# Opening of a two-block model on one core: k/v weight chunks moved to even distance among the adaLN chunks

## What is computed

```python
shift, scale, gate = jnp.split(jax.nn.silu(c) @ ada_w[l] + ada_b[l], 3, axis=-1)
shift_c, scale_c, gate_c = jnp.split(jax.nn.silu(c_ctx) @ ada_w[l] + ada_b[l], 3, axis=-1)
h = rmsnorm(x, norm_g[l]) * (1.0 + scale[:, None]) + shift[:, None]
hc = rmsnorm(xc, norm_g[l]) * (1.0 + scale_c) + shift_c
qc, kc, vc, upc, ufc, gc = split_proj(hc @ w_in[l])
q, k, v, up, uf, g = split_proj(h @ w_in[l])
```

## Time and profile before

| | |
|---|---|
| median of three runs | 2354.19 us (2352.36 to 2354.57) |
| the profiled execution, its own time | 2351.8 us |
| its span in the trace | 2350.0 us |
| TensorE busy | 2269.2 us (97%) |
| VectorE / ScalarE / GpSimd busy | 1290.6 / 1040.8 / 267.9 us |
| HBM read and written | 428.89 MB and 6.29 MB |
| mean granted clock of TensorE | 0.988 |

### The profile page before, as it was taken

How to read it: one execution, slowest core, us unless ns; L and a number is a source line. 1 busy time by engine, 2 the same in 40 slices (tenths; PEclk the granted TensorE clock), 3 DMA queues, 4 the chain that set the end, 5 groups by cost and what they waited for, 6 DMA issues and landing times.

```text
span 2350.0 us, 30042 instructions
## 1 busy us (share of the span) xinstructions
PE 2269.2 (97%) x11859; PEld 1831.6 (78%) x11859; DVE 1290.6 (55%) x2038; ACT 1040.8 (44%) x1602; POOL 267.9 (11%) x326
## 2 busy tenths in 40 slices
PE   5899999999999999999999998999999999999998
PEld 2477777777777866678888886888888888888887
DVE  3354533332332264545776767677755777567764
ACT  2233333332322254445554465555544555345553
POOL 1000100000010122100020324111100111001111
PEclk8999999999999999999999999999999999999999
DMA  9964433444655485734566544565555555656553
GB/s 355 349 241 166 149 126 114 137 138 161 244 179 171 135 280 178 244 99 159 182 199 206 171 152 153 179 194 182 189 195 191 185 186 186 197 188 188 187 189 117
DMA packets 322427, 437.14 MB, mean 186 GB/s; under 512 B 13848, under 2 KB 220112, under 8 KB 321264
## 3 DMA queue, kind: packets, MB, share of 16 engines
q1 hardware_dynamic: 316800, 413.19, 53.3%
q0 software_dynamic: 3392, 16.90, 1.9%
q10 hardware_dynamic: 2096, 5.15, 0.6%
HBM read 428.89 MB, written 6.29 MB: 185 GB/s over the span
## 4 chain that ended last, share of the span: by engine, by line
PE 88%; DVE 4%; ACT 3%; DMA 2%; issue 1%; POOL 1%; SPq 0%; ACTq 0%; POOLq 0%
PE ps L1332 24%; PE ps L1333 12%; PE ps L1307 9%; PE ps L1309 9%; PE ps L1308 9%; PE ps L1327 5%; PE ps L1329 5%; PE ps L1328 5%; PE ps L1287 3%; PE ps L1381 1%; ACT SPL L1538 1%; DVE SPL L1781 1%; PE ps L1398 1%; DMA RAW<-in_w_in_dram 1%; DMA RAW<-in_ada_w_dram 1%
## 5 line engine op out<-in xcount | busy, mean ns | idle before, releaser
L1781 DVE TENSOR_TENSOR SPL<-RAW,SPL 128x1024 fp32r<-128x1024 f32 x592 | 752.7, 1274 | 618.3 <-ACT SPL L1538 615.6
L1332 PE MATMUL ps<-HS,SPL 128*128 128x512 f32 x2688 | 954.4, 400 | 12.3 <-DVE SPL L1781 9.5
L1538 ACT ACTIVATE SPL<-RAW 128x1024 fp32r<-128x1024 f32 x592 | 622.1, 1055 | 492.3 <-PE ps L1309 171.6
L1333 PE MATMUL ps<-HS,SPL 128*128 128x256 f32 x2688 | 755.5, 281 | 0.0
L1332 PEld LDWEIGHTS ps<-HS,SPL 128*128 128x128 f32 x2688 | 507.2, 189 | 135.8 <-DVE SPL L1781 8.4
L1333 PEld LDWEIGHTS ps<-HS,SPL 128*128 128x128 f32 x2688 | 510.4, 190 | 2.0 <-issue 1.7
L1307 PE MATMUL ps<-SPL,HS 128*128 128x512 f32 x960 | 398.5, 415 | 15.5 <-POOL HS L2232 5.6
L1309 PE MATMUL ps<-SPL,HS 128*128 128x512 f32 x960 | 379.3, 395 | 0.0
L1308 PE MATMUL ps<-SPL,HS 128*128 128x512 f32 x960 | 379.1, 395 | 0.0
L1307 PEld LDWEIGHTS ps<-SPL,HS 128*128 128x128 f32 x960 | 183.3, 191 | 78.8 <-issue 24.7
L1308 PEld LDWEIGHTS ps<-SPL,HS 128*128 128x128 f32 x960 | 183.6, 191 | 41.5 <-issue 6.0
(11 more groups left out here) (281 smaller groups left out, 1684.9 us busy)
## 6 DMA issues: line engine op xcount, KB each, us to landing
RAW<-in_w_in_dram SPq DMA_DIRECT2D x208, 512.0 KB, 5.7
RAW<-in_ada_w_dram SPq DMA_DIRECT2D x192, 512.0 KB, 4.9
RAW<-in_ffn_w_up_dram SPq DMA_DIRECT2D x192, 512.0 KB, 3.5
RAW<-in_w_out_dram SPq DMA_DIRECT2D x96, 512.0 KB, 4.4
RAW<-in_ffn_w_down_dram SPq DMA_DIRECT2D x96, 512.0 KB, 3.8
x_spill<-XT POOLq DMA_DIRECT2D x2, 2048.0 KB, 15.1
XT<-x_spill POOLq DMA_DIRECT2D x1, 4096.0 KB, 16.9
MM<-in_x_dram ACTq DMA_DIRECT2D x2, 1024.0 KB, 11.0
```

The lines of the kernel that those rows point to most:

```text
L1332: mm(PS[b][:, :], wr, hh, start=k == 0, stop=False, skip_group_check=True)
L1333: m = mm(PS[b][:, 256:512], wl, hh[:, 0:256], start=False, stop=k == KT - 1, skip_group_check=True)
L1538: act(SPL[:, (n - 1) % NSPL, 0, :], raw_of(i), ACT.Copy).then_inc(s_hi, 1)
L1781: tt(w[:, 1, :], raw_of(s["i"]), w[:, 0, :].bitcast(F32), ALU.subtract).then_inc(s_lo, 1)
```

## The change

The k/v chunks of steps 1 to 3 are put after the eighth and the sixteenth adaLN chunk of a step in place of the twelfth and the sixteenth. (`cs` holds sixteen adaLN chunks; `kv[2u - 1:2u]` stands after all of them in both versions.) They come to stand at 24 and 33, 42 and 51, 60 and 69, 70 and 71: eight adaLN chunks between any two of the first six. The number of side steps popped with every second adaLN chunk, which was 2 for chunks 0 to 7, 4 for 8 to 27 and 2 from 28 on, becomes 4 from chunk 8 on.

```diff
                 if c.shape == 0:
-                    pop_side((2 if i < 8 or i >= 28 else 4) if c.group.side == 2 and c.kc % 2 == 0 else 0)
+                    pop_side((2 if i < 8 else 4) if c.group.side == 2 and c.kc % 2 == 0 else 0)
...
                 cs[-1].then = start_h
-                return cs[:12] + kv[2 * u - 2:2 * u - 1] + cs[12:] + kv[2 * u - 1:2 * u] if u else cs
+                return cs[:8] + kv[2 * u - 2:2 * u - 1] + cs[8:] + kv[2 * u - 1:2 * u] if u else cs
```

## The result

The kernel after takes 2363.43 us (median of five runs, 2361.82 to 2367.48), the kernel before 2354.19 us: a ratio of 1.0046, with a 95% interval of 1.0035 to 1.0057, or 9.2 us more. The profiled execution of the kernel after took 2363.4 us, its span is 2361.6 us. One execution of this study, of the kernel after with the old number of side steps, took 3236 us at a granted clock of 0.65 and is left out of all figures.

The account below looks back on a forecast made before the run. TensorE was taken to bound the kernel, so an opening shift passes to the end one for one. Terms -0.5 + 2.9 + 9.7 = +12.1 us gave 2366 us; range 2352 to 2371 us.

Parts of the forecast that it names:

- Rival A: Opening: cycle as computed, but the clock drops only for kv0 and at most once more; +0.4 to +4.3 us, chance 0.20.
- Rival C: Opening's end set by something both kernels have, the spill or the h tiles; shift below 2 us, 2354, chance 0.09.
- kv0: First k/v chunk, moved from 28 to 24: lands at 52.1 us, starts at 55.7 in place of 59.92.
- The cycle: Eight adaLN chunks, one k/v chunk: next k/v chunk starts 7.6 us after the eight begin; 13.76 us per cycle.
- the landing: Restarted w_in load, issue to landing: 4.1 us taken, bounded below by 3.7.
- The lower bound of 3.7: Least landing time from 20 to 130 us; at it the five cycles would give 2.0 us back.
- kv5 without the clock: Start of kv5 with no clock effect: 124.5 us against 125.02 before, -0.5 us.
- The clock: Drops at six idle times of 3.8 us or more, ahead of kv0 to kv5: 2.9 plus 9.7, 12.6 us.
- the tail: After kv5 (h tiles of step 3, kv6, kv7, copies out): same list in both versions, so its length stays.
- kv5 near 137 us: Sign in the profile after that would show the forecast right: kv5 near 137 us.
- At nothing: Terms priced at zero in the opening, among them four side steps in place of two.
- Rival B: DMA stream closes up if restart loads land in 2.5 us; kv5 starts at 115.3, -8 us, 2346, chance 0.15.

Follow-up runs that it names:

- the second profile: Profile of the kernel after run once more, unchanged, beside three others: 2362.03 us, ratio 1.0043 against the kernel before.

## Why the prediction was right

The forecast was +12.1 us and 2366 us; measured were +9.2 and 2363.4. The sign and the mechanism stand, and each link of the chain is in the trace; two of its terms and one of its grounds were off. The range, 2352 to 2371 us, was wide enough to hold rivals A and C too, so it is the steps that count. By those steps, against the trace after:

- *kv0* was put at 55.7 us and started at 56.02, behind the seventh high part of the h tiles as said.
- *The cycle.* From the start of the eight adaLN chunks to the next k/v chunk I had 7.6 us. Measured were 7.27, 7.18, 7.43, 7.16 and 6.99, 7.2 in the mean. The term that was off is the landing: 4.1 taken, 3.50 to 3.95 measured. The lower bound of 3.7 was the better one in this execution; in the kernel after with the old number of side steps they took 3.73 to 4.04. That these loads find the engines idle, where the one of 4.1 us had a share of 0.57 around it, does not explain it: in the run with matmuls in the idle time, loads that were issued behind a microsecond with a share of 1.06 and 0.96 landed in 3.72 and 3.69 us, one behind a share of 0.00 in 3.85, and two behind 1.07 and 0.50 in 4.71 and 4.36. So 4.1 us lies within the scatter, and its cause stays open. The estimate of 3.2 us from the Trainium skill, page "DMA: Bandwidth & Descriptors", section "Anatomy of one DMA", which the page gives for the GpSimd path, is too low for these loads of SyncE. Over the five cycles that is -2.0 us, and kv0's start gives 0.3 back: kv5 without the clock at 133.16 - 10.3 = 122.9 in place of 124.5.
- *The clock* was the main term, 12.6 us. Over 6.16 us, kv0 to kv4 took 2.0, 2.8, 1.6, 2.5 and 1.5 us more, 10.3 together, and kv5 to kv6 took 10.05 us, 2.6 more than before: 12.9. The run with matmuls in the idle time shows the cause. The forecast of six drops came true in this execution, but its ground did not: I had six idle times of 3.8 us or more, each longer than the one of 3.74 us that came with a drop, and four of the five ahead of kv1 to kv5 are shorter than that (3.34 to 3.63 us). That the clock dropped at all of them is in part luck; the second profile has four drops in six.
- *What I left out*: the drop that the kernel before has from 134.5 to 138 us lies in the tail, which I had called the same in both. It is not there in the profile after: from kv6 to the mark it takes 13.1 us in place of 14.7. That is -1.6 us. It is no work of the change: the kernel after with the old number of side steps has 15.0 us there, the kernel before with the new number 13.1, behind the same two idle times of 1.2 and 0.6 us. So that this execution was spared it is luck; a row with its price was there, and the sum had it at nothing in both kernels.
- *The sum* of what was measured: 122.9 - 125.0 = -2.1, +10.3, +2.6, -1.6, in all +9.2 us, and the mark moved by 9.1. I also wrote "kv5 near 137 us", where my own terms give 124.5 + 2.9 + 4 x 1.9 = 135.0; it came at 133.2.
- *At nothing* were the side steps: both runs on them show it.
- Rival A (the clock holds) is out, though a single execution can come halfway to it. Rival B (the stream closes up) is what the kernel does as soon as it has the buffers: kv5 starts at 116.0 us where 115.3 was worked out, and the total is 2345.8 where it was 2346, though B reached its numbers by a shorter landing and not by more buffers. With eight buffers its point of decision is not reached, 3.5 us being the least landing time and 2.5 what it asked. Rival C is out, the mark moved by the whole loss.

On the clock the Trainium skill, page "TensorE: Matmul & The Clock Gate", section "HAM oscillation", says that a loop which waits for its next slice falls back to the low clock in each round. The trace after agrees with it in all five rounds from kv1 to kv5, the second profile in three of five.

## What to carry to other kernels

With a ring of n load buffers, look at what frees the buffer of the item that is on the critical path: here the k/v chunk stood n + 1 places behind the last one, so its own load was gated by the first thing TensorE does after the last one, and even spacing was the bad spacing; distances of eight and ten by turns were no better, though, and what helped was one buffer more. A wait of a few microseconds ahead of a block of large matmuls cost its own length here and, where the clock dropped, 1.3 to 2.9 us more in the block behind it. Before moving work between resources, look for idle memory: four buffers in a tile that is unused during the opening brought 0.31 to 0.35% against the kernel before in either order, while the orders themselves came to the same.

## What was not expected of the hardware

An idle time of 3.83 us ahead of kv2 left TensorE's clock at 1.00, while 2.66 us in the kernel before and 3.34 us in the kernel after dropped it to 0.50; the length of the idle time alone does not decide. The 512 KB load that gates a k/v chunk landed in 3.50 to 3.95 us in the kernel after and in 3.69 to 4.71 us in the run with matmuls in the idle time, and the DMA share just before it does not order these times. The restart in the run with distances of eight and ten reached only 282 GB/s from 68 to 72 us, against 387 to 392 elsewhere, for a cause that stays open in part.
